# Stick-breaking attention turned on its side: queries on partitions, a backward prefix scan on VectorE for the sums over later keys, and the weights turned by TensorE

## What is computed

```python
z = jnp.einsum('bhqd,bhkd->bhqk', qb.astype(jnp.float32), kf) * scale
causal = key_pos[None, :] < q_pos[:, None]
log_beta = jax.nn.log_sigmoid(z)
log_keep = jnp.where(causal, log_beta - z, 0.0)
between = lax.cumsum(log_keep, axis=3, reverse=True) - log_keep
w = jnp.where(causal, jnp.exp(log_beta + between), 0.0)
return jnp.einsum('bhqk,bhkd->bhqd', w, vf)
```

## Time and profile before

| | us |
|---|---|
| median of 3 runs | 3287.08 |
| range of the runs | 3281.28 to 3287.86 |
| the profiled execution's own span | 3281.4 |
| fastest timed run, 0.1 below that span | 3281.28 |
| the stage, first logits to first convolution product | 80.5 to 470.4, 389.9 |

### The profile page before, as it was taken

One profiled execution on the slowest core, in us unless ns is written; L12 is line 12 of the kernel. 1 busy time (PEld: TensorE's weight loads), 2 busy tenths in 40 slices (PEclk: granted clock), 3 DMA queues, 4 the chain that ended last, 5 costly groups with the idle time before them and its releaser, 6 DMA issues.

```text
span 3281.4 us, 35513 instructions
## 1 busy us (share of the span) xinstructions
PE 3009.6 (92%) x13882; PEld 2446.4 (75%) x13882; DVE 1776.3 (54%) x1774; ACT 1236.8 (38%) x1951; POOL 1052.0 (32%) x418
## 2 busy tenths in 40 slices
PE   5888899999989999999989999999988899989996
...
GB/s 100 20 26 33 26 85 50 52 45 52 90 32 52 45 52 45 52 45 52 58 45 45 129 52 68 84 20 20 20 84 39 84 26 33 26 26 26 78 109 64
DMA packets 42567, 171.59 MB, mean 52 GB/s; under 512 B 4464, under 2 KB 5488, under 8 KB 41392
## 3 DMA queue, kind: packets, MB, share of 16 engines
...
...
## 4 chain that ended last, share of the span: by engine, by line
PE 72%; DVE 11%; issue 10%; ACT 5%; POOL 1%; DMA 0%; ACTq 0%; SPq 0%; DVEq 0%; POOLq 0%
PE ps L513 45%; PE ps L1141 5%; PE ps L904 3%; PE aux L1032 3%; PE ps L694 2%; PE ps L967 2%; PE ps L1016 2%; PE ob L1058 1%; PE aux L723 1%; PE ob L1061 1%; DVE eb L2029 1%; PE ob L1059 1%; PE ps L714 1%; DVE pw_l L1876 1%; DVE zb L2007 1%
## 5 line engine op out<-in xcount | busy, mean ns | idle before, releaser
L456 POOL TENSOR_TENSOR wh<-raw,con 128x1024 fp32r<-128x1024 f32 x203 | 492.1, 2424 | 2159.2 <-PE ps L513 936.1
L458 POOL TENSOR_TENSOR wl<-raw,wh 128x1024 fp32r<-128x1024 f32 x203 | 552.1, 2720 | 15.9
L513 PE MATMUL ps<-hh,wh 128*128 128x512 f32 x1344 | 422.4, 396 | 25.3 <-POOL wl L458 15.2
L513 PE MATMUL ps<-hl,wh 128*128 128x512 f32 x1344 | 419.1, 393 | 0.0
L513 PE MATMUL ps<-hh,wl 128*128 128x512 f32 x1344 | 418.4, 393 | 0.0
L513 PEld LDWEIGHTS ps<-hh,wh 128*128 128x128 f32 x1344 | 255.3, 191 | 82.0 <-POOL wl L458 16.9
L513 PEld LDWEIGHTS ps<-hl,wh 128*128 128x128 f32 x1344 | 256.1, 191 | 54.2
L513 PEld LDWEIGHTS ps<-hh,wl 128*128 128x128 f32 x1344 | 255.4, 190 | 53.8
L1876 DVE TENSOR_TENSOR px_l<-px,px_h 128x512 fp32r<-128x512 f32 (+3 forms) x288 | 205.3, 714 | 121.4 <-ACT px_h L1690 119.4
L1393 ACT ACTIVATE ff<-fr 128x1024 f32<-128x1024 f32 x32 | 34.0, 1061 | 553.6 <-DVE fr L2120 553.6
L2131 DVE TENSOR_TENSOR y_t<-y_t,ps 128x1024 f32<-128x1024 f32 x120 | 146.4, 1220 | 173.0 <-PE ps L513 173.0
...
## 6 DMA issues: line engine op xcount, KB each, us to landing
...
xold_t<-spill_x ACTq DMA_DIRECT2D x2, 4096.0 KB, 13.2
...
x_t<-xt ACTq DMA_DIRECT2D x1, 4096.0 KB, 12.9
...
```

Source lines behind the costliest of these rows:

```text
L456: pool.tensor_tensor(wh[:, s, :, :], raw[:, s, :, :], ones.unsqueeze(1).broadcast_to([P, KT, P]), ALU.mult).then_inc(w_high, 1)
L458: pool.tensor_tensor(wl[:, s, :, :], raw[:, s, :, :], wh[:, s, :, :].bitcast(F32), ALU.subtract).then_inc(w_split, 1)
L513: m = pe.matmul(ps[:, w, a:b], lw[:, sl, k, :], r[:, i, a:b], start=(i == 0 and j == 0), stop=(i == len(ks) - 1 and j == 2))
```

## The change

The stage is turned. Queries lie on the partitions, keys along the row. A unit is one block of 128 queries (`qi` = 0 to 7) against all keys up to its end, (qi+1)*128 columns: both heads in one unit for qi 0 to 3, one head a unit for qi 4 to 7, again 12 units a pair and 48 in all. Their row lengths are 256, 512, 768, 1024 (two heads together), then 640, 640, 768, 768, 896, 896, 1024, 1024. The causal cut is added by one matmul with `cut_r` (0 or -2^100) into the logits. The sums over later keys become one `tensor_tensor_scan` a head on VectorE, run backward along the row and in place. So sp needs no split, no `suffix`, no mask, no cap and no copy of z: the logits stay in PSUM, alternating between `ps` slot 0 and `aux` (`zs`), until VectorE has subtracted. The weights then have queries on the partitions while the value product needs keys there, so PE turns them: `turn` transposes blocks of 128x128, up to four at a time (a tile), into bank `TURN` of `ob`; ScalarE and VectorE split them from there; `av` runs 3 matmuls of 128 columns for each block. A tile is turned only when the one before has left the bank. One of the nine convolution products is moved into the end of the stage.

```diff
@@ -157,12 +155,10 @@
-    zb = [at(18 + i, f"zb{i}", [P, 2, HALF], F32) for i in range(3)]
-    pw_l = [at(18 + i, f"pw_l{i}", [P, 2, HALF], F32R) for i in range(3)]
-    eb = [at(21 + i, f"eb{i}", [P, 2, HALF], F32) for i in range(3)]
-    sp_l = [at(21 + i, f"sp_l{i}", [P, 2, HALF], F32R) for i in range(3)]
-    sp_h = [at(24 + i, f"sp_h{i}", [P, 2, HALF], F32R) for i in range(2)]
-    pw_h = at(26, "pw_h", [P, 2, HALF], F32R)
+    eb = [at(18 + i, f"eb{i}", [P, S], F32) for i in range(3)]
+    wb = [at(21 + i, f"wb{i}", [P, S], F32) for i in range(2)]
+    pw_h = [at(23 + i // 2, f"pw_h{i}", [P, HALF], F32R, 2048 * (i % 2)) for i in range(4)]
+    pw_l = [at(25 + i // 2, f"pw_l{i}", [P, HALF], F32R, 2048 * (i % 2)) for i in range(4)]
...
-                first = min(max(kb * P - chunk * HALF, 0), HALF - 256)
-                SB_UNITS.append((pair, chunk, kb, first, HALF - first))
+        SB_UNITS += [(pair, qi, (0, 1)) for qi in range(4)]
+        SB_UNITS += [(pair, qi, (h,)) for qi in range(4, 8) for h in range(2)]
     NU = len(SB_UNITS)
+    PER_PAIR = NU // SB_PAIRS
+    SB_TILES, FIRST_TILE = [], []
+    for u, (pair, qi, heads) in enumerate(SB_UNITS):
+        FIRST_TILE.append(len(SB_TILES))
+        blocks = [(h, kb) for h in heads for kb in range(qi + 1)]
+        SB_TILES += [(u, blocks[i:i + 4]) for i in range(0, len(blocks), 4)]
+    FIRST_TILE.append(len(SB_TILES))
+    def sb_tiles(u):
+        return range(FIRST_TILE[u], FIRST_TILE[u + 1]) if 0 <= u < NU else range(0)
+    def sb_columns(u):
+        _, qi, heads = SB_UNITS[u]
+        return [(h, HALF * i, (qi + 1) * P) for i, h in enumerate(heads)]
...
+        return 4 * pair + qi // 2
...
         def logits(u):
-            if u > 0:
-                pe.wait_ge(z_free, u)
-                if u % (NU // SB_PAIRS) == 0:
-                    pe.wait_ge(piece_free, 4 * (pair - 1) + 2)
-            for h in range(2):
-                for j, (a, b) in enumerate(((0, 0), (1, 0), (0, 1))):
-                    q0 = chunk * HALF + first
-                    m = pe.matmul(ps[:, Z_SLOT, h * HALF:h * HALF + n], k[a][:, kb * P:(kb + 1) * P],
-                                  q[b][:, h, q0:q0 + n], start=(j == 0), stop=(j == 2))
+            if u >= 2:
+                pe.wait_ge(d_ready, u - 1)
+            if u > 0 and u % PER_PAIR == 0:
+                pe.wait_ge(piece_free, 4 * (pair - 1) + 2)
+            k, q, z = ks[pair % 2], pads[pair % 2], zs[u % 2]
+            for h, at_, n in sb_columns(u):
+                for j, (a, b) in enumerate(((0, 0), (0, 1), (1, 0))):
+                    for c in range(0, n, HALF):
+                        e = min(c + HALF, n)
+                        pe.matmul(z[:, at_ + c:at_ + e], q[a][:, h, qi * P:(qi + 1) * P], k[b][:, c:e],
+                                  start=(j == 0), stop=(j == 2 and e < n), skip_group_check=True)
+                m = pe.matmul(z[:, at_ + n - P:at_ + n], id_r[:, :], cut_r[:, :], start=False, stop=True, skip_group_check=True)
...
-        def suffix(u, tri):
-            first, n = SB_UNITS[u][3:]
-            for h in range(2):
-                for r in (sp_h[u % 2], sp_l[u % 3]):
-                    m = pe.matmul(aux[:, h, first:first + n], tri[:, :], r[:, h, 0:n],
-                                  start=False, stop=True, skip_group_check=True)
+        def turn(t_):
+            u, blocks = SB_TILES[t_]
+            pe.wait_ge(pw_ready, u + 1)
+            if t_ > 0:
+                pe.wait_ge(pwl_ready, t_)
+            for j, (h, kb) in enumerate(blocks):
+                at_ = HALF * SB_UNITS[u][2].index(h) + kb * P
+                m = pe.transpose(ob[:, TURN, j * P:(j + 1) * P], wb[u % 2][:, at_:at_ + P], ident)
+            m.then_inc(tr_done, 1)
...
-            for h in range(2):
-                for a, r in ((0, pw_h), (1, pw_h), (0, pw_l[u % 3])):
-                    m = pe.matmul(ob[0:64, h, first:first + n], v[a][:, kb, h * 64:(h + 1) * 64], r[:, h, 0:n],
-                                  start=False, stop=True, skip_group_check=True)
+            for j, (h, kb) in enumerate(blocks):
+                at_ = 256 * h + qi % 2 * P
+                for i, (a, r) in enumerate(((0, pw_h), (1, pw_h), (0, pw_l))):
+                    m = pe.matmul(ob[0:64, OUT, at_:at_ + P], v[a][:, kb, h * 64:(h + 1) * 64], r[t_ % 4][:, j * P:(j + 1) * P],
+                                  start=(kb == 0 and i == 0), stop=(kb == qi and i == 2), skip_group_check=True)
...
-        clear(aux)
-        for step in range(NU + 3):
-            if step >= 3:
-                av(step - 3)
-            if 2 <= step < NU + 1:
-                u = step - 2
-                pe.wait_ge(d_ready, u + 1)
-                if first_of_chunk(u + 1):
-                    clear(aux).then_inc(rest_done, 1)
-                else:
-                    suffix(u, rest_r).then_inc(rest_done, 1)
-            sb_part(step)
-            if step + 1 < NU:
-                logits(step + 1)
-            if 1 <= step <= NU:
-                pe.wait_ge(spl_ready, step)
-                suffix(step - 1, tri_r).then_inc(tri_done, 1)
-        pe.wait_ge(z_free, NU)
+        for step in range(NU + 2):
+            tiles = sb_tiles(step - 2)
+            for n, t_ in enumerate(tiles):
+                turn(t_)
+                if t_ > 0:
+                    av(t_ - 1)
+                if n == 0:
+                    sb_part(step)
+                    if step + 1 < NU:
+                        logits(step + 1)
+            if not tiles:
+                sb_part(step)
+                if step + 1 < NU:
+                    logits(step + 1)
+            if step == NU:
+                pe.wait_ge(d_ready, NU)
+                product(range(KT), hh, hl)
+        av(len(SB_TILES) - 1)
         pe.wait_ge(piece_free, 4 * (SB_PAIRS - 1) + 3)
-        for j in range(1, CONV_TILES):
+        for _ in range(2):
...
+        def high_tile(t_):
+            m = len(SB_TILES[t_][1]) * P
+            act.wait_ge(tr_done, t_ + 1)
+            if t_ >= 4:
+                act.wait_ge(av_done, t_ - 3)
+            copy(pw_h[t_ % 4][:, 0:m], ob[:, TURN, 0:m]).then_inc(pwh_ready, 1)
...
-                copy(sp_h[m % 2][:, :, 0:nm_], eb[m % 3][:, :, 0:nm_]).then_inc(sph_ready, 1)
...
+                e = sb_view(a, eb[a % 3][:, :])
+                act.activation(e, sb_view(a, zs[a % 2]), ACT.Abs).then_inc(abs_ready, 1)
+            if tiles:
+                high_tile(tiles[0])
...
+                w_ = sb_view(b, wb[b % 2][:, :])
+                act.activation(w_, w_, ACT.Exp).then_inc(pw_ready, 1)
+            if len(tiles) > 1:
+                high_tile(tiles[1])
...
+        def low_tile(t_):
+            m = len(SB_TILES[t_][1]) * P
+            dve.wait_ge(pwh_ready, t_ + 1)
+            low(pw_l[t_ % 4][:, 0:m], ob[:, TURN, 0:m], pw_h[t_ % 4][:, 0:m]).then_inc(pwl_ready, 1)
...
-                d = dve.tensor_tensor(z[:, :, 0:n], z[:, :, 0:n], aux[:, :, first:first + n], ALU.subtract)
-                if kb >= 4 * chunk:
-                    chain(d)
-                    c0, c1 = (0, 256) if kb == 4 * chunk + 3 else (0, P)
-                    cap = con[:, C_CAP + 256 - c1:C_CAP + 256].unsqueeze(1).broadcast_to([P, 2, c1])
-                    d = dve.tensor_tensor(z[:, :, c0:c1], z[:, :, c0:c1], cap, ALU.min)
-                d.then_inc(d_ready, 1)
-            if 0 <= m < NU:
-                n = SB_UNITS[m][4]
-                dve.wait_ge(sph_ready, m + 1)
-                low(sp_l[m % 3][:, :, 0:n], eb[m % 3][:, :, 0:n], sp_h[m % 2][:, :, 0:n]).then_inc(spl_ready, 1)
+                e = eb[b % 3]
+                dve.wait_ge(sp_ready, b + 1)
+                for h, at_, n in sb_columns(b):
+                    back = e[:, at_:at_ + n][:, ::-1]
+                    i = dve.tensor_tensor_scan(out=back, data0=ones[:, 0:1].broadcast_to([P, n]), data1=back, initial=0.0,
+                                               op0=ALU.mult, op1=ALU.add)
+                i.then_inc(scan_ready, 1)
+                dve.wait_ge(scan_ready, b + 1)
+                if b >= 2:
+                    dve.wait_ge(tr_done, FIRST_TILE[b - 1])
+                dve.tensor_tensor(sb_view(b, wb[b % 2][:, :]), sb_view(b, zs[b % 2]), sb_view(b, e[:, :]),
+                                  ALU.subtract).then_inc(d_ready, 1)
+            if tiles:
+                low_tile(tiles[0])
...
-                dve.tensor_copy(z[:, :, 0:n], zsrc[:, :, 0:n]).then_inc(z_free, 1)
...
-                    i = dve.tensor_tensor(e[:, :, 0:c1], e[:, :, 0:c1], mask, ALU.mult)
-                i.then_inc(sp_ready, 1)
...
+                e = sb_view(a, eb[a % 3][:, :])
+                dve.scalar_tensor_tensor(out=e, in0=sb_view(a, zs[a % 2]), scalar=0.0, in1=e,
+                                         op0=ALU.max, op1=ALU.add).then_inc(sp_ready, 1)
+            if len(tiles) > 1:
+                low_tile(tiles[1])
```

148 lines of the change are left out of this document (52 added, 96 removed).

## The result

The changed kernel takes **3233.47 us** (median of 4 runs, 3228.07 to 3236.58) against 3287.47 us (also 4 runs; the table of the kernel before has three of them); the ratio is 0.9833, with a 95% interval of 0.9818 to 0.9848. Forecast were 3239.6 us and a range of 3205 to 3275. Here is the head of the page after, which answers to the earlier trace rows.

What follows compares the result with a forecast made beforehand. PE was taken to bound the kernel: 75.3 (PE's loop) + 5.8 + 1.5 + 3 = 85.6 us a pair, a stage of 342.4 against 389.9, 47.5 less, so 3239.6 us from the median; range 3205 to 3275 (8 in 10).

Steps and rivals of the forecast that it cites:

- PE's work, 72.7 a pair: PE in the turned stage: logits 13.2, turns 7.9, filler 32.8, turns of v 0.7, value product 18.1 us a pair.
- the price that I had to choose: Value product on PE: 0.084 us per 128-column matmul, between 0.058 and 0.11; 216 matmuls make 18.1 us a pair.
- PE's work before, 76.8 a pair and "4.1 under now": PE's counted work in the old stage, 76.8 of 96.9 us a pair; the turned stage's work was put 4.1 lower.
- The second tile's round trip: PE waits for the second tile's high and low copies: 12.7 us a pair, 10.1 given back by hidden products.
- before second turns: Sign of being right: PE would wait for `pw_l` before second turns, 1 to 1.6 us each.
- VectorE longer than PE: Where VectorE's list outlasts PE's loop: 5.8 us a pair (q step 3.8, last unit 1.1, two small units 0.9).
- GpSimd, 3 us a pair: VectorE's scans meet the end of GpSimd's splits: 1 us a slab, 3 a pair, bounds 0 and 5.1 a slab.
- The tail, zero within 3: Stage's end: moved product (10.9 us) fills waits, but bare turns cost some 4 and slot 0 maybe 2; taken as zero.
- the waits hide: Rival, 0.14: the second tile's copies overlap more and no scan meets GpSimd; 78 us a pair, 3209 us.
- the first tile's round trip is not free: Rival, 0.12: if all 22 tiles a pair wait like second ones, 97.6 us a pair, 3288 us, no change.
- the clock falls: Rival, 0.06: waits in each unit leave PE at 1.2 GHz; a third of the stage so gives 3325 us.
- The dearer scan: Rival, 0.06: VectorE's backward in-place scan takes twice as long, 102 us a pair, 3353 us; decides from 1.6 times.

Runs made afterwards that it cites:

- The two kernels without splits: Kernel before and changed kernel, each with GpSimd splitting only 2 of 128 columns of 12 slabs in the stage: 3260.54 us and 3234.68 us.
- tail_back: Changed kernel with the moved convolution product put back behind the stage: 3235.5 us, ratio 0.9832 to the kernel before.
- filler_ahead: Changed kernel with filler pieces that continue a slab (eight of twelve steps) put ahead of the step's first turn on PE: 3259.53 us.
- low_behind_scan2: Changed kernel, filler ahead of first turns except positions 5 and 9 (behind the last), ScalarE's list reordered, second low part behind the next scan: 3273.67 us.
- scan_twice: Changed kernel with an idle scan of the same length ahead of each real scan on VectorE: 3309.74 us, ratio 1.0054 to the kernel before.

## Why the prediction was right, and where its terms were off

**The mechanism held.** PE's work, its waits for `pw_l`, VectorE's q step and the end of GpSimd's interference give the time; the forecast was 3239.6, measured 3233.47. That the two are 6 us apart is in part luck, since misses cancel. Per pair, PE's work came out 2.2 us above its term and the second tile's wait 1.8 above, VectorE's waits 2.3 below and GpSimd's share nearly all of its 3 below.

**PE's work, 72.7 a pair.** I added up, in the second pair (378 rows of PE from 159.8 to 243.8 us), the distances from each start to the next, less the idle that rows name: logits 14.5 (13.2 forecast), turns 6.6 (7.9), value products 17.0 (18.1), filler 35.2 (32.8; 1.4 of it the slow matmuls behind the wait for q), turns of v 1.6 (0.7). Sum 74.9, 2.2 above. The value product, the price that I had to choose, came out at 17.0 / 216 = 0.079 against 0.084: 0.060 in a stream, more at each tile's first and last. The Trainium skill's 81 ns (TensorE: Matmul & The Clock Gate, "Back-to-back issue gap") agrees with that mean, and not with the distance inside a stream, 60 ns.

**PE's work before, 76.8 a pair and "4.1 under now".** This count does not enter the sum, but it was 8 us too low. In the third pair before, PE's named waits are 11.6 us, so 96.9 - 11.6 = 85.3 are its own time; after it is 84.0 - 9.4 = 74.6. PE saves some 10.7 us a pair and not 4.1, and the waits before were 12 us a pair and not 20.

**The second tile's round trip.** Forecast: 12.7 us a pair, 10.1 hidden, so 2.6 exposed. Measured: 4.4 in the second pair and in the third. (The 19.5 us of the stage hold one wait of 2.9 at 407.71 us, in the last unit but one. There a first tile's low part stands in VectorE's list behind the last unit's scan and subtraction, with no filler and no logits left on PE to cover it.) The hidden part was too large: with the stream at 0.060, the first tile's product covers 12 x 0.06 + 0.08 = 0.80 us and not 1.01, ten of them 8.0; 12.7 - 8.0 = 4.7, near the 4.4 if the round trips themselves were right, which I did not add up. The waits stand in front of the next unit's first turn, which I had put as "before second turns"; they are 0.55 us each on average in these pairs and not 1 to 1.6.

**VectorE longer than PE.** Forecast 5.8 and 1.5 for v, 7.3; the third pair has 5.0 us of such waits on PE: 3.0 for q, 0.7 for k, 1.3 for the sums. The place (the step that takes q) was right.

**GpSimd, 3 us a pair.** This is the term that was most off: 2.3 us of VectorE's time in the whole stage and not 12. At that size the forecast would have been 3230. The step that failed is who waits. A split did begin during a scan, as I had written, in six of twelve slabs, but then GpSimd stood (high parts of 2.78 to 3.50 us instead of 2.40) and was through before the next scan; only the scans of one small unit were held up. No scan of 1024 columns was, where I had named one in four. The two kernels without splits confirm both ends: 21.7 us (marker) before, 0.6 after.

**The tail, zero within 3.** `tail_back` gives -2.1 by the marker and +2.0 by the medians, which agree within their intervals. Its parts came as written: the two bare turns and the last product 4.9 us (4 forecast), slot 0 1.8 us (2).

**The rivals.** That the waits hide (3209) is out: 32.2 us of them stand. That the first tile's round trip is not free did not come: ScalarE's wait for logits is 14.8 us, and first tiles' turns are covered by filler and logits; `filler_ahead`, which takes the filler from between the turns in eight steps of twelve, is 23.2 us longer. That the clock falls did not come here (0.97), but the disturbed orders show that it is real: 0.90 over the stage of `low_behind_scan2`, where PE has waits of up to 6.3 us and its matmuls took 19.7 us longer. The Trainium skill (same page, Part 4) says that turning does not count as busy for the clock; with 288 turns in the stage the granted clock stayed at 0.97, so nothing here speaks for that as a cost.

The dearer scan did not come (2281 ns), and `scan_twice` shows what it would have cost: 3309.7 us. My figure for it, 3353, does not follow from its own sum. The sum written there, 102 us a pair, gives 4 x 102 = 408, 18 more than 389.9, hence 3306; measured is (336 + 80.9) / 4 = 104 a pair. Its mechanism was not all there: 29 us of the cost are PE at a lower clock. The point from which it decides is, on a straight line between the two measurements, 1 + 54 / 81 = 1.67, against my 1.6.

**Not settled.** The medians give GpSimd 32 us of the gain and the profiles 22; that the difference is the spread behind the marker is likely from its size and was not tested. Why the clock drops more in one order than in another was seen only beside the waits, and not varied by itself.
